# Half of the last group's fourth product behind the first chunk's outputs, the second chunk's keys turned ahead of them, and a gate behind the squares, in an mLSTM layer on one core

## What is computed

```
def mlstm_mixer(u, w_in, b_if, norm_g, w_out):
    q, k, v, o_pre, if_pre = jnp.split(u @ w_in, ...)
    def step(carry, inp):
        ...
        scores = einsum('bhtd,bhsd->bhts', qc, kc) * exp(log_d - m_t)
        num = w_inter * einsum('bhtd,bhde->bhte', qc, c_st) + einsum('bhts,bhse->bhte', scores, vc)
        h = num / max(|den|, exp(-m_t))
        w_k = exp(log_w - m_new) * kc
        c_st = decay * c_st + einsum('bhsd,bhse->bhde', w_k, vc)
        ...
    h = merge_heads(_rms(from_blocks(h))) * norm_g
    return (h * jax.nn.sigmoid(o_pre)) @ w_out
...
h = h + mlstm_mixer(rmsnorm(h), ...)
h = h + (silu(u @ w_gate) * (u @ w_up)) @ w_down        # u = rmsnorm(h)
```

## Time and profile before

| what | value |
|---|---|
| median of 3 runs | 2117.95 us (2116.78 to 2119.38) |
| the profiled execution's own time | 2117.55 us |
| its span (first to last instruction) | 2115.9 us |
| PE busy | 2080.2 us (98% of the span) |
| DVE busy | 1427.1 us (67%) |
| ACT busy | 920.7 us (44%) |
| chain that ended last, share of PE | 92% |

### The profile page before, as it was taken

One profiled execution on the slowest core, in us unless ns is written; L12 is line 12 of the kernel. 1 busy time (PEld: TensorE's weight loads), 2 busy tenths in 40 slices (PEclk: granted clock), 3 DMA queues, 4 the chain that ended last, 5 costly groups with the idle time before them and its releaser, 6 DMA issues.

```text
span 2115.9 us, 28683 instructions
## 1 busy us (share of the span) xinstructions
PE 2080.2 (98%) x10088; PEld 1720.9 (81%) x10088; DVE 1427.1 (67%) x2252; ACT 920.7 (44%) x1646; POOL 228.4 (11%) x334
## 2 busy tenths in 40 slices
PE   6999989999999999999999999999999999999999
PEld 5888878888888888888888888788888888888887
DVE  8764578786575665679677545878857566566764
ACT  5433664353333333445444347544533333334443
POOL 3200100111010010100111001002101001010000
PEclk9999999999999999999999999999999999999999
DMA  4423477212323325773424236862232332357443
GB/s 151 135 86 120 150 273 225 90 61 99 120 100 103 99 99 176 257 253 115 154 65 160 80 110 195 272 203 68 75 120 95 103 105 99 118 190 243 155 134 105
DMA packets 221405, 294.23 MB, mean 139 GB/s; under 512 B 13488, under 2 KB 148656, under 8 KB 221296
## 3 DMA queue, kind: packets, MB, share of 16 engines
q1 hardware_dynamic: 192944, 195.66, 29.5%
q0 software_dynamic: 28352, 97.15, 12.9%
HBM read 210.31 MB, written 82.44 MB: 138 GB/s over the span
## 4 chain that ended last, share of the span: by engine, by line
PE 92%; DVE 3%; ACT 2%; DMA 2%; issue 1%; POOL 0%; SPq 0%; DVEq 0%; POOLq 0%; ACTq 0%
PE ps L2420 13%; PE ps L2423 13%; PE ps L2422 13%; PE ps L2468 7%; PE ps L2470 7%; PE ps L2472 7%; PE ps L2184 4%; PE ps L2188 4%; PE ps L2186 4%; PE ps L2059 3%; PE ps L2061 3%; PE ps L2060 3%; PE ps L2150 2%; PE ps L2151 2%; PE ps L2152 2%; PE ps L2066 2%
## 5 line engine op out<-in xcount | busy, mean ns | idle before, releaser
L1897 DVE TENSOR_TENSOR ring<-raw_f,ring 128x512 fp32r<-128x512 f32 x308 | 211.2, 687 | 188.2 <-ACT ring L1271 187.3
L1271 ACT CAST ring<-raw_f 128x512 fp32r<-128x512 f32 x308 | 191.1, 622 | 208.8 <-PE ps L2423 193.2
L2420 PE MATMUL ps<-u_lo,ring 128*128 128x512 f32 x704 | 275.7, 392 | 0.0
L2423 PE MATMUL ps<-u_hi,ring 128*128 128x512 f32 x704 | 274.1, 389 | 0.0
L2422 PE MATMUL ps<-u_hi,ring 128*128 128x512 f32 x704 | 273.9, 389 | 0.0
L2468 PE MATMUL ps<-ring,ring 128*128 128x512 f32 x616 | 240.5, 390 | 0.8 <-DVE ring L1976 0.8
L2470 PE MATMUL ps<-ring,ring 128*128 128x512 f32 x616 | 239.7, 389 | 0.0
L2472 PE MATMUL ps<-ring,ring 128*128 128x512 f32 x616 | 239.7, 389 | 0.0
L2420 PE MATMUL ps<-t_op,ring 128*128 128x512 f32 x528 | 206.0, 390 | 0.0
L2423 PE MATMUL ps<-t_op,ring 128*128 128x512 f32 x528 | 205.5, 389 | 0.0
L2422 PE MATMUL ps<-t_op,ring 128*128 128x512 f32 x528 | 205.4, 389 | 0.0
(11 more groups left out here) (226 smaller groups left out, 4137.3 us busy)
## 6 DMA issues: line engine op xcount, KB each, us to landing
ops_hbm<-kept POOLq DMA_DIRECT2D x154, 256.0 KB, 2.4
g_in<-ops_hbm SPq DMA_DIRECT2D x154, 256.0 KB, 2.7
raw_f<-in_ffn_w_gate_dram SPq DMA_DIRECT2D x44, 512.0 KB, 4.7
raw_f<-in_ffn_w_up_dram SPq DMA_DIRECT2D x44, 512.0 KB, 4.5
b<-in_ffn_w_down_dram SPq DMA_DIRECT2D x88, 256.0 KB, 4.4
raw<-in_ml_w_in_dram SPq DMA_DIRECT2D x16, 1024.0 KB, 5.4
proj_hbm<-pkept POOLq DMA_DIRECT2D x64, 256.0 KB, 2.9
x_in<-in_x_dram SPq DMA_DIRECT2D x16, 512.0 KB, 6.4
```

What stands on the lines that cost most here:

```text
L1271: nc.scalar.copy(four(ring[slot][:, 0, :]), feed_source(q, s)).then_inc(w_hi_done, 1)
L1897: nc.vector.tensor_tensor(four(ring[slot][:, 1, :]), feed_source(q, s), four(ring[slot][:, 0, :].bitcast(F32)), ALU.subtract).then_inc(w_l ...
L2420: pe.matmul(banks(bank), wh, moved(kind, 1, k), start=(fresh and k == 0), stop=False, skip_group_check=True)
L2423: last = pe.matmul(banks(bank), wl, moved(kind, 0, k), start=False, stop=(k == 3), skip_group_check=True)
```

## The change

The change touches only the start of the chunk stage, once in each half of the tokens. The second half of unit 82 moves behind `outputs(0)`; unit 83 is no longer cut; `turn_keys(1)` moves from the middle of unit 83 to a place ahead of `outputs(0)`, which needs a free accumulator bank (0 in place of 3) and second buffers `kw_second` and `qw_second` for chunk 1; `state_sums(1)` moves ahead of `turn_heads(0)`. On DVE the keys and queries of chunk 1 are weighed behind the scores of chunk 0, and `weigh_queries(2)` moves ahead of `add_out(0, 0)`. On ACT the copy of unit 82 and its gate (`keep_unit` and `sigmoid(PG - 1, 2, 3)`) move behind `squares(0)`, and the eight decays of chunk 1 stand together. On SP `qkc` goes ahead of `v1` for chunk 0, `negb(2)` ahead of `qkc(2)`, and the 1 MB transfer `load_wo(1, 1)` and `load_v(2)` move behind `load_og(1)`. On POOL `load_res(0)` moves behind the last store of the group.

```
@@ SP
                 sp.wait_ge(v_stored, h * 64 + 64)
-                load_v(0)
                 sp.wait_ge(p_fed, h * PU + unit_at(11, 2) + 1)
                 load_qkc(0)
+                load_v(0)
                 load_wo(1, 0)
                 sp.wait_ge(p_fed, h * PU + unit_at(11, 4) + 1)
                 load_qkc(1)
                 load_v(1)
-                load_wo(1, 1)
+                load_negb(2)
                 load_qkc(2)
-                load_negb(2)
                 sp.wait_ge(p_stored[1], h * 224 + 224)
                 sp.wait_ge(p_first_stored, h * 16 + 16)
                 load_og(0)
-                load_v(2)
                 load_wq(2)
                 load_og(1)
+                load_v(2)
+                load_wo(1, 1)
                 load_qkc(3)
@@ POOL
-                            if g == PG - 1 and k == 1:
-                                pool.wait_ge(p_fed, h * PU + PU - 1)
-                                load_res(0)
                             pool.wait_ge(o_gated, done + 3 + i)
                             store_block(g, k)
+                        if g == PG - 1:
+                            pool.wait_ge(p_fed, h * PU + PU - 1)
+                            load_res(0)
@@ ACT
-                    if n > 6 and not is_value(n):
+                    if n > 6 and not is_value(n) and n != PU - 2:
                         keep_unit(g, q)
...
-                        if q == 6:
-                            sigmoid(g, 2, 3)
...
                     squares(c)
                     if c == 0:
-                        decay_matrix(1, 0, 4)
+                        keep_unit(PG - 1, 6)
+                        sigmoid(PG - 1, 2, 3)
                     head_rstd(c)
                     if c == 0:
-                        decay_matrix(1, 4, HEADS)
+                        decay_matrix(1)
                         sigmoid(PG - 1, 3, 1)
@@ DVE
                 for c in range(TILES):
+                    if c == 0 or c >= 3:
+                        weigh_queries(c)
                     if c != 1:
-                        weigh_queries(c)
-                    weigh_keys(c)
-                    if c == 1:
-                        weigh_queries(c)
+                        weigh_keys(c)
                     weigh_scores(c)
                     if c == 0:
                         split_out(1, 0)
                         split_out(1, 1)
+                        weigh_keys(1)
+                        weigh_queries(1)
...
                     head_scale_b(c)
...
+                    if c == 1:
+                        weigh_queries(2)
                     if c:
                         add_out(c - 1, 0)
@@ PE
                 project(PU - 2, 0, 2)
                 scores(0)
+                state_sums(0)
+                turn_keys(1)
+                outputs(0)
                 project(PU - 2, 2, 4)
-                state_sums(0)
-                outputs(0)
-                project(PU - 1, 0, 2)
-                turn_keys(1)
-                project(PU - 1, 2, 4)
+                project(PU - 1)
                 scores(1)
+                state_sums(1)
...
                     turn_heads(c - 1)
...
-                    state_sums(c)
+                    if c > 1:
+                        state_sums(c)
                     outputs(c)
```

More of the change, by code:

```diff
@@ L486, in t4_made, with kw_of, qw_of, key_bank @@
             return stage * 8 + (2 * p + 2 if stage % 2 or p == 0 else 5 + p)
+        def kw_of(c):
+            return kw_second if c == 1 else kw
+        def qw_of(c):
+            return qw_second if c == 1 else qw
+        def key_bank(c):
+            return 0 if c == 1 else 3
         def value_source(kind, k):
@@ L2273, in turn_keys @@
                 def turn_keys(c):
[L2275 removed]
+                    if c >= 2:
                         pe.wait_ge(state_done, h * 32 + c * 4)
[L2277 to L2279 removed]
+                    else:
                         pe.wait_ge(qkc_loaded[c % 2], h * 64 + 16 * (c // 2) + 16)
                     for g in range(4):
[L2282 removed]
+                        last = pe.transpose(ps[:, key_bank(c), g * P:g * P + P], qkc[c % 2][:, 4 + g, :], ident[:, :])
                     last.then_inc(k_turned, 1)
```

37 lines of the change are left out of this document (19 added, 18 removed).

## The result

The changed kernel takes 2122.53 us in the median of 8 runs (2119.73 to 2125.12), the kernel before 2117.95 us beside it (8 runs, 2116.78 to 2119.38). The ratio is 1.0021, with a 95% interval of 1.0012 to 1.0029: slower by 4.6 us, just past the 0.2% that a measurement of this kernel can tell. The profiled execution took 2121.16 us, with a span of 2119.4 against 2115.9: 3.5 us of the 4.6 are in the two traces.

The account below looks back on a forecast made before the run. PE, busy 98% of the span, bounds the kernel; its waits allow about 9 us. First half -1.6 + 0.9, second +0.5 + 0.9: +0.7 us on 2117.55 gives 2118.3, as median 2118.6, range 2115.5 to 2122.5.

Parts of the forecast that it names:

- The chain that I followed: Start of chunk stage: gate block 3 on ACT, its store, the load of og(0), 3.7 us of DVE, then PE.
- the clock: Behind PE's merged wait a low-clock stretch meets out_tile(0, 0): 0.9 us lost per half, bounds 0 and 1.5.
- the pair of transfers: Gate block 3's store plus the load of og(0): 6.4 us in a nearly idle queue, bounds 6.2 and 14.1.
- the long wait at L2073: Sign: one long wait of PE at out_tile's first line, 3 us and more in each half.
- the shorter one at L2357: Sign: a shorter wait of PE at the turning of the heads; about 1.5 of 2.44 us go.
- the quick store: Sign: POOL's store of gate block 3, near 283.9 and 1330.5, lands in under 4 us.
- the half microsecond at L2294: Sign: a wait of PE at turn_keys for qkc, about half a microsecond.
- The keys' load: Load of chunk 1's keys lands in 5.0 us, at 275.1, so outputs(0) starts 0.5 us earlier in the first half.
- the 0.36 us wait of chunk 0: PE's wait for chunk 0's load may go, but only lengthens the wait for chunk 1's keys: worth nothing.
- chunk 1's keys come late: Rival: keys landing in 7.0 us instead of 5.0 make each half 2 us later, 2122.6; slower outcomes together 0.15.
- The gate behind the squares: Gate block 3 behind chunk 0's squares on ACT: its store is issued 6.1 us later, at 283.9 in the first half.
- if the residual came after 302: Residual issued near 289, wanted near 302; if later, DVE would stand ahead of chunk 2's weighing, one for one.

Follow-up runs that it names:

- e10: Changed kernel with the load of chunk 0's values back ahead of SP's wait, so ahead of chunk 0's keys and queries: 2119.12 us, ratio 1.0006.
- e2: Changed kernel with og(0) loaded from rows stored long before, so it need not wait for gate block 3's store: 2116.69 us, ratio 0.9995.
- e7: Changed kernel with 20 transposes of the identity on PE ahead of out_tile(0, 0), in the wait for og(0): 2120.33 us, ratio 1.0014.
- e1: Changed kernel with the second half of unit 82 and gate block 3 back in their old places, new transfer order kept: 2120.89 us, ratio 1.0015.
- e4: Changed kernel with the transposes of chunk 1's keys moved behind outputs(0) on PE: 2120.43 us, ratio 1.0014.
- e9: Changed kernel with chunk 1's keys loaded ahead of the 1 MB of weights, DVE's split of these behind chunk 1's weighing: 2119.00 us, ratio 1.0005.
- e11: Changed kernel with half of unit 82 and gate block 3 back, residual load sooner, 18 identity transposes ahead of chunk 0's heads: 2114.94 us, ratio 0.9985.
- e12: Kernel before with the changed transfer order, residual load behind gate block 3's store landing, 18 identity transposes ahead of chunk 0's heads: 2114.85 us, ratio 0.9982.
- e3: Kernel before with only the changed order of SP's and POOL's transfers: 2116.40 us, ratio 0.9990.

## Why the prediction was off

I forecast no measurable change, 2118.6, and +0.7 us for both halves; the stages grew by 3.7 us. The chain that I followed was the right one, with one term wrong. That the forecast came out as near as it did is luck of the margin: the ratio is 0.21% where I had put the limit at 0.2%, and the median stands 0.03 us above the top of my range, whose width was meant for the clock and the pair of transfers and had no room for late keys. Of the signs that I had written down, the long wait at L2073, the shorter one at L2357 and the quick store came; the half microsecond at L2294 was 1.47 and 1.70 us. Each half splits at the points of the table:

| part | half 1, predicted | measured | half 2, predicted | measured |
|---|---|---|---|---|
| `outputs(0)` against before | -0.5 | +0.54 | -0.9 | +0.76 |
| from `outputs(0)` to `out_tile(0, 0)` | -1.1 | -1.18 | +1.4 | +1.60 |
| from there to `out_tile(1, 0)` (clock) | +0.9 | +0.99 | +0.9 | +1.03 |
| stage | -0.7 | +0.35 | +1.4 | +3.39 |

(-1.1 is the gain of 1.6 at `og(0)` less the 0.5 that the outputs come earlier; 1.4 is 0.5 lost and 0.9 likewise.)

**The keys' load: the step that failed.** I took the 5.0 us of the kernel before for the new order, because "what is ahead in the queue is the same 2 MB as before". It is, and still the load took 6.0 and 6.2. The 1.0 and 1.7 us of the first line are 2.7 of the 3.0 us by which the sum is off. e10 shows the cause to be the swap of `v1` and `qkc`, which I had priced at "worth nothing" for the other end of it, the 0.36 us wait of chunk 0. For the second half I wrote that I had no row and took the outputs 0.9 us earlier. The trace of the kernel before has one, for its load issued at 1317.07:

```profile
qkc<-proj_hbm SPq DMA_DIRECT2D x1, 512.0 KB, 4.6
```

With 0.6 us of transposes this landing gives just those 0.9 us. The new load landed 1.6 us later in its stage, and that is nearly all of the 1.7; in the first half it landed 1.0 us later, and the outputs missed by 1.0. With this one term put right, as in e10, the two stages are 0.4 us longer than before, where my sum had +0.7. The rival "chunk 1's keys come late" was the true one. It had its mechanism and its price per microsecond, and was put aside with the argument on bytes. Its 2122.6 was worked out for a landing 2 us late in each half; it was 1.0 and 1.6 us late, so that the median comes so close to that number only with the microsecond below.

**The pair of transfers: right.** Store and load took 2.7 + 3.6 = 6.3 us in the first half, 6.6 in the second; I had 6.4 from the idle end of the earlier trace rows. The fit of the Trainium skill ("DMA: Bandwidth & Descriptors", "Anatomy of one DMA — SWDGE (gpsimd) path") gave an estimate of 2.6 us for the store, and the trace agrees with 2.7.

**The gate behind the squares: right.** The store went out at 284.66 and 1332.18, 283.9 and 1330.5 predicted; the differences are the late outputs. That waiting for it is the dear part is shown by e2: 6.2 us for both halves with the clock.

**The clock: right, in both halves.** 1.0 us per half against 0.9, and e7 shows it by taking it away.

**What costs nothing.** The residual and `wo_raw(1, 1)` were hidden in the changed kernel, as said, but only by the wait for `og(0)`: in e1 and e2, where that wait is gone, the residual was next. The prediction named this ("if the residual came after 302") and gave it no price.

**The 1 us that one profile lacks.** The median grew by 4.6 us, the profiled execution by 3.6. The runs of the changed kernel spread over 5.4 us, those with a mean granted clock of 0.994 took 2124.3 and 2125.1, the one with 0.999 took 2119.7; but one with 0.998 took 2123.7. I think that low stretches in other waits of the stage make up the rest; the executions above the profiled one have no trace here, so this is argued, not shown.

## What to carry to other kernels

When a wait is filled or removed, write down for each of the things due next (the load behind it, the residual, the next keys) when it lands, and take the latest; e1 won 2 us at the point aimed at and lost them 11 us later. The landing time of a load depended here on the order of its queue, not only on the bytes ahead: before a load is put on the critical path, price it by its slowest row, rather than by the old order's. And an in-order queue passes a wait on even when the first engine is relieved of it (e4): move the waiting instruction on each engine that holds it.

## What the runs showed of the hardware

Two loads swapped in one queue, with the same bytes ahead of a third, changed its time to landing from 4.4 and 4.8 us to 6.0 and 6.2 (e10 against the changed kernel), and that of the 1 MB of weights between them from 7.0 to 8.5 in the first half. Over the 13 profiles that have one of the two orders they don't overlap: 4.4 to 5.0 us in six halves, 5.5 to 7.3 in twenty.

A wait of PE did not decide alone whether the granted clock fell behind it. It fell after 2.44 us in the first half of the kernel before and not after 2.43 in the second; after 1.82 us in e7; and not after 3.21 and 3.06 us in the second halves of e4 and e9, from where the next 13.40 us ran at full clock. Idle transposes of the identity in the wait, 18 of them in 2.15 us, were followed by full clock in all four halves in which they stood ahead of the heads, and e11 and e12 are the fastest kernels of the study. Their runs spread over 2.9 and 2.3 us, those of the changed kernel over 5.4; but those of e3, without filler and with a low stretch in both halves, spread over 2.6, so the narrow spread is not shown to come from the filler.
